# The splits of the weight tiles move from ahead of a job's post-treatment to behind it, at most four tiles ahead, in a three-block float32 network on one core

## The reference, cut to what matters

```python
def swiglu(x, w_in, w_out):
    gate, up = jnp.split(x @ w_in, 2, axis=-1)
    return (jax.nn.silu(gate) * up) @ w_out
...
    qkv = x @ w_qkv
    q, k, v = jnp.split(qkv, 3, axis=-1)
...
    for i in range(s // Q_BLOCK):
        sc = jnp.einsum('bqhmd,bkhmd->bhmqk', q[:, q0:kend], k[:, :kend],
                        preferred_element_type=jnp.float32)
        p = jax.nn.softmax(jnp.where(allowed, sc, neg), axis=-1)
        a = p[:, :, 0] - lam * p[:, :, 1]
        outs.append(jnp.einsum('bhqk,bkhe->bqhe', a.astype(v.dtype), v[:, :kend]))
```

## Time and profile before

| | |
|---|---|
| runs | 1912.24 us median of 3 (1912.19 to 1922.69) |
| profiled execution | 1916.28 us, span of the instructions 1914.6 us |
| mean granted TensorE clock | 0.984 |
| busy | PE 96%, DVE 47%, ACT 35%, POOL 3% |
| chain that ended last | PE 90%, DVE 5%, ACT 3%, issue 2% |

### The profile page before, as it was taken

How to read it: one execution, slowest core, us unless ns; L and a number is a source line. 1 busy time by engine, 2 the same in 40 slices (tenths; PEclk the granted TensorE clock), 3 DMA queues, 4 the chain that set the end, 5 groups by cost and what they waited for, 6 DMA issues and landing times.

```text
span 1914.6 us, 21555 instructions
## 1 busy us (share of the span) xinstructions
PE 1841.1 (96%) x8656; PEld 1480.3 (77%) x8656; DVE 903.6 (47%) x1544; ACT 664.8 (35%) x1084; POOL 57.9 (3%) x68
## 2 busy tenths in 40 slices
PE   8987879999999999999999999999999999999998
PEld 6755557888888897566698888888887788888886
DVE  3576766533333362555573333336544474334343
ACT  4233432422223232555432232222446444323231
POOL 0221110000000000000000000000000000000000
PEclk9989899999999999999999999999999999999999
DMA  7321111423333323222223333333321324333221
GB/s 235 98 77 49 66 53 56 132 77 112 98 99 99 120 87 107 66 67 67 83 89 99 93 95 99 99 98 96 100 73 60 110 67 122 99 100 99 77 78 44
DMA packets 217306, 174.51 MB, mean 91 GB/s; under 512 B 8899, under 2 KB 177765, under 8 KB 217206
## 3 DMA queue, kind: packets, MB, share of 16 engines
q1 hardware_dynamic: 217206, 173.13, 29.7%
HBM read 170.97 MB, written 7.38 MB: 93 GB/s over the span
## 4 chain that ended last, share of the span: by engine, by line
PE 90%; DVE 5%; ACT 3%; issue 2%; DMA 0%; SPq 0%; ACTq 0%
PE ps L526 27%; PE ps L527 27%; PE ps L528 27%; PE ps L823 2%; PE ps L783 2%; ACT whi L989 1%; PE ps L803 1%; PE ps L833 1%; PE ps L845 1%; PE ps L722 1%; DVE wlo L1263 1%; PE ps L793 0%; PE ps L934 0%; DVE arena L1289 0%; DVE arena L1285 0%
## 5 line engine op out<-in xcount | busy, mean ns | idle before, releaser
L1263 DVE TENSOR_TENSOR wlo<-raw,whi 128x1024 fp32r<-128x1024 f32 x236 | 288.3, 1225 | 588.8 <-ACT whi L989 586.6
L989 ACT ACTIVATE whi<-raw 128x1024 fp32r<-128x1024 f32 x236 | 248.8, 1059 | 578.3 <-PE ps L528 570.8
L526 PE MATMUL ps<-xh,whi 128*128 128x512 f32 (+1 forms) x1176 | 444.9, 378 | 0.0
L528 PE MATMUL ps<-xh,wlo 128*128 128x512 f32 (+1 forms) x1176 | 433.2, 368 | 0.0
L527 PE MATMUL ps<-xl,whi 128*128 128x512 f32 (+1 forms) x1176 | 433.1, 368 | 0.0
L526 PE MATMUL ps<-whi,hh 128*128 128x512 f32 x648 | 257.1, 397 | 7.2 <-DVE hl L1467 3.8
L526 PEld LDWEIGHTS ps<-xh,whi 128*128 128x128 f32 x1176 | 224.0, 190 | 39.0 <-issue 4.6
L528 PE MATMUL ps<-whi,hl 128*128 128x512 f32 x648 | 253.8, 392 | 0.0
L527 PE MATMUL ps<-wlo,hh 128*128 128x512 f32 x648 | 253.6, 391 | 0.0
L528 PEld LDWEIGHTS ps<-xh,wlo 128*128 128x128 f32 x1176 | 223.2, 190 | 37.4
L527 PEld LDWEIGHTS ps<-xl,whi 128*128 128x128 f32 x1176 | 223.6, 190 | 36.7 <-issue 2.9
(11 more groups left out here) (198 smaller groups left out, 2021.7 us busy)
## 6 DMA issues: line engine op xcount, KB each, us to landing
raw<-in_ffn_w_in SPq DMA_DIRECT2D x88, 512.0 KB, 3.9
raw<-in_w_ff SPq DMA_DIRECT2D x64, 512.0 KB, 4.0
raw<-in_ffn_w_out SPq DMA_DIRECT2D x44, 512.0 KB, 3.8
raw<-in_a_w_qkv SPq DMA_DIRECT2D x24, 512.0 KB, 5.2
raw<-in_w_in SPq DMA_DIRECT2D x20, 512.0 KB, 3.8
raw<-in_kv_w SPq DMA_DIRECT2D x16, 512.0 KB, 3.7
bias_skewed<-bias_rows SPq DMA_DIRECT2D x8, 640.0 KB
raw<-in_a_w_o SPq DMA_DIRECT2D x8, 512.0 KB, 4.7
```

What stands on the lines that cost most here:

```text
L526: e.matmul(o, ah, bh, start=start, stop=False)
L528: return e.matmul(o, al, bh, start=False, stop=stop)
L989: e.activation(self.parts(m)[0], self.raw[:, m % RAW, :], ACT.Copy).then_inc(s.hi, 1)
L1263: e.tensor_tensor(lo, self.raw[:, m % RAW, :], f32(hi), ALU.subtract).then_inc(s.lo, 1)
```

## The change

`done` no longer calls `pump`. `post` calls `pump(1)` behind its own step. The limit falls from eight tiles ahead of the last one taken (`SPLIT + EXTRA`) to four (`AHEAD`). As `slots` is a queue from which the first is taken, and as two of six slots (four of eight) are now left over, a split gets the slot that has been free the longest, mostly that of the job before the last one.

```diff
@@ -22,6 +22,7 @@
 SPLIT = 6
 EXTRA = 2
+AHEAD = 4
@@ -88,7 +89,7 @@
     def pump(self, most=2):
 
-        while most and self.slots and not self.waiting and self.n_split < len(self.tiles) + SPLIT + EXTRA:
+        while most and self.slots and not self.waiting and self.n_split < len(self.tiles) + AHEAD:
             slot, free = self.slots.pop(0)
@@ -108,7 +109,6 @@
         if self.slot_of[tile] < SPLIT or self.extra:
             self.slots.append((self.slot_of[tile], (sem, value)))
-        self.pump()
@@ -145,6 +145,7 @@
         else:
             self.step("post", job, None)
+        self.pump(1)
```

## The result

The changed kernel took 1869.99 us, the median of 4 runs (1866.1 to 1872.17), against 1914.38 us for the kernel before beside it (4 runs, 1912.19 to 1922.69): a ratio of 0.9758 [0.9722, 0.9794], faster by 44 us or 2.4%. The forecast was 1877.0 us with a range of 1862 to 1898. The profiled execution took 1871.5 us, with a span of 1869.8 us, where the one before had 1914.6 us.

What follows compares the result with a forecast made beforehand. TensorE, busy 96%, bounds the kernel; its idle time and low clock, mainly in the first attention, can be won. 25.6 + 8 - 3 + 4 = 34.6, rounded to 35 us: 1881 us profiled, 1877 us median, range 1862 to 1898.

Steps and rivals of the forecast that it cites:

- What bounds the kernel: Whole kernel: TensorE busy 96%; feed-forwards can gain nothing, the gain lies in the attentions' waits and low clock.
- The waits on the post: First attention: each post begins 2.35 us earlier, so ten waits on its last operation, 32.6 us, shrink by 21.9 us.
- The shares and maxima: First attention: two waits on the shares' L1459 shrink by 2.2 us, one on the maxima's L1126 by about 1.5.
- the splits' new places: First attention: splits beside GpSimd's addition or ahead of shares cost 3 us, about 0.2 for each of 14 jobs.
- The clock: First attention: five or six of eleven clock falls left, 1.7 us each; 9.4 us won, 8 of it real.
- The second attention: Second attention: waits on L1490 shrink and part of one clock fall goes, 4 us; shares 1.3 us later are covered.
- Fewer tiles ahead: Norms and loads: splitting four tiles before use instead of six or more costs nothing; else L526 would wait on wlo.
- the clock and the coupling keep half: Rival, chance 0.17: in the first attention each shortened wait lets the next grow; gain 15 to 20 us, about 1894.
- the wait only moved: Rival, chance 0.05: split delays the next head's maxima; first attention gains nothing, second loses 18 us and more, 1930.
- nothing comes of it: Rival, chance 0.04: post starts earlier but TensorE's waits end with another releaser at the same time, 1905 to 1915.
- GpSimd and VectorE lock each other out: Rival, chance 0.06: 11 first-attention splits each wait for GpSimd's 1.27 us addition, giving back 14 us; 1891.

Runs made afterwards that it cites:

- e3: Changed kernel with the split put back directly ahead of the post, at most five tiles ahead there, so in an older slot: 1887.18 us.
- e1: Changed kernel with the old limit of eight tiles ahead; the split stays behind the post but takes the slot just freed: 1871.38 us.
- e2: Changed kernel with only the limit of four kept; `done` calls `pump` again and `post` doesn't: 1871.86 us.
- e4: Changed kernel with each PSUM bank chosen as the one given back longest ago, instead of the next in turn: 1868.41 us.
- e7: Changed kernel with VectorE's half of every split done twice: 1941.7 us.

## Why the prediction was right, point by point

**What bounds the kernel: right.** The feed-forwards kept their length, TensorE busy throughout. All but 2.3 of the 44.8 us came in the two attentions.

**The waits on the post, 21.9 us: right.** 32.6 fell to 10.2 us, by 22.4. The price of 2.35 us per wait was 2.41 where it can be read alone (4.69 to 2.28, and 3.38 to 0.97). The three forecast to stay above 2 us did, at 2.28, 2.28 and 2.18. The reason given for the price was incomplete: it took both halves in series as one cause, and e3 shows two.

**The shares and maxima, 2.2 + 1.5, and the splits' new places, -3: right, each for itself.** The two waits on L1459 fell from 5.4 to 2.6 us, by 2.85 where 2.2 was taken, and the one on L1126 from 2.9 to 1.6, by 1.3 where 1.5 was taken. Five new waits on the shares came in their place, 3.4 us together: that is the subtraction of 3 us. In all 25.6 - 3 = 22.6 us were forecast, and TensorE's idle time fell by 23.1.

**The clock, 8 us: the mechanism right, the size wrong.** The term was forecast at 8 us and measured 12.8. The price of a fall was right (1.7 taken, about 1.5 measured). The step that failed is the count: "I take five or six falls to be left", and then 8 of 9.4 "real". In the trace of the kernel before, the eleven falls stood behind ten waits of 2.47 to 4.69 us and one of 1.89, and none behind a shorter one. My own list left three waits above 2 us and the rest under about 1.5, so it allowed three falls at most. There were two, one and one in three traces of this order.

**The second attention, 4 us: the cause right, the size too small.** It gave 6.5 us: 4.3 of idle time (7.7 to 3.4) and 2.2 of busy time. I had taken 2 of the 3.7 us of its four longer waits; nearly all went (4.9 to 0.5 in total). The cause is the one given, shares that no longer stand behind a split; but it takes the limit of four to get there, since a split right behind the post still stands ahead of them and gives only 3.3 us (e1). The 1.3 us by which the next shares come later were covered, as forecast: no wait of L834 stands there.

**The mixer: missed.** 2.1 us came that were not in the sum. One wait of 1.85 us on the mixer's hl (L1574) is 0.3 us now, which is 1.6 of them. The fall of the clock behind it (at 1518.58 us) is gone, and another stands earlier in the mixer (at 1382.27). Why that wait shrank I have not traced.

**Fewer tiles ahead, at nothing: right.** No wait of L527 on wlo stands in a feed-forward or at a norm; the one in the trace is that at the start, 3.0 us in both.

**What the change is.** The title and the first sentences on the change give the move to the call in `post`; with the limit of four the limit does it (e2). The order of the engines, from which the terms were read, was right, so no number hung on it.

**The rivals.** That the clock and the coupling keep half: no, but e4 and e7 show the coupling it feared, in the 22 us that are left. That the wait only moved: no; in the second attention L834 waits 0.5 us once. That nothing comes of it: no. That GpSimd and VectorE lock each other out: the lock is there, and its price was already being paid. GpSimd's addition in the first attention, before and then after:

```profile
L1603 POOL TENSOR_TENSOR arena<-arena 128x512 f32<-128x512 f32 x14 | 17.8, 1270 | 141.2 <-DVE arena L1289 141.2
```

```profile
L1604 POOL TENSOR_TENSOR arena<-arena 128x512 f32<-128x512 f32 x13 | 22.4, 1720 | 98.7 <-DVE arena L1290 98.6
```

In e1, where a split stands behind nearly every post, the mean is 2111 ns for each of 13. Who loses is seen in two places. In e1 the split began first, and GpSimd took 2.13 us, 0.99 us of them up to the split's end at 138.41:

```profile
137.19 1.22 DVE L1264 TENSOR_TENSOR wlo<-raw,whi 128x1024 fp32r<-128x1024 f32 x1
...
137.42 2.13 POOL L1604 TENSOR_TENSOR arena<-arena 128x512 f32<-128x512 f32 x1 [12.23 <-DVE arena L1290]
```

In the changed kernel GpSimd was once the first, by 0.05 us, and the split took 2.30 us:

```profile
103.66 1.27 POOL L1604 TENSOR_TENSOR arena<-arena 128x512 f32<-128x512 f32 x1 [0.28 <-DVE arena L1290]
103.71 2.30 DVE L1264 TENSOR_TENSOR wlo<-raw,whi 128x1024 fp32r<-128x1024 f32 x1 [0.20 <-ACT whi L990]
```

The Trainium skill (SBUF — State Buffer, "Who interferes with whom") says that the order of issue decides which of the two blocks, and that the other blocks fully. These two places agree: the later one ended 1.14 us and 1.08 us after the first had ended, near the length it has alone. The place at 83.77 in the earlier trace rows does not: GpSimd's L1608 was the first by 0.56 us there, and the split kept its 1.23 us. The prediction quoted the rule's first half and priced VectorE as the loser each time; at most places the split begins right behind the post's last operation, some 0.2 us ahead of GpSimd, which is released by that operation.

But VectorE pays one operation later. The shares' L1456 reads two operands from SBUF and takes 0.16 us alone; in four places it began while GpSimd's addition ran, took 1.05 us, and ended within 0.02 us of it:

```profile
97.74 2.13 POOL L1604 TENSOR_TENSOR arena<-arena 128x512 f32<-128x512 f32 x1 [10.64 <-DVE arena L1290]
...
98.84 1.05 DVE L1456 TENSOR_TENSOR stat<-stat,small 128x1 f32<-128x1 f32 x1
```

TensorE's wait of 1.31 us at 101.44 ends with the shares behind this row. Added up, the first attention of the changed kernel loses 4 x 0.9 us of VectorE so, 2 x 1.0 at the next line (L1457, 1.5 us instead of 0.5) and 1.1 at the one split, some 6.7 us. The kernel before lost 6 x 1.0 us at that next line (its L1456, as in the earlier trace rows). So hardly anything was given back, where the rival had 14 us.

**The total.** 34.6 us forecast, 44.8 in the profiled execution: 23.1 for 22.6, 12.8 for 8, 6.5 for 4, 2.1 for 0, and 0.3 elsewhere.

## What to carry to other kernels

Work done ahead for later use belongs behind the treatment of a result in every engine's order, and into a buffer that is free already: the place and the buffer are two separate delays. In the first attention an older buffer alone was worth 15 us and the place 21 or more beyond that, and behind the post the buffer counted for nothing (e1); in the second either was enough, if the place was behind the next results as well. A limit on how far ahead a planner works can decide both, so look at the order that comes out, not at the line that was moved. When waits are priced, count also what the clock loses behind each one that is removed, and ask whether the next result of the same engine is late by as much: giving TensorE another bank here only showed it the next late result. And when an operation is doubled to see what it costs, look up how long the second one took: here it was 1.71 us and not 1.22.

## What the runs showed of the hardware that I had not expected

A wait of 2.28 us of TensorE at the same matmul of the same order was followed by the granted clock's lower level in one execution and not in another (two, one and one falls in three traces of the changed order; none and one in two of e1's). Longer waits are not sure to be followed by one either: of the kernel before, the wait of 2.92 us that ended at 277.48 had none, and one of 1.89 us, ending at 213.72, had one. A fall costs TensorE about 1.5 us. So two orders cannot be told apart in a single trace where they differ by 3 us in a stage with such waits.

GpSimd's addition, 1.27 us alone, took 2.0 to 2.1 us in 13 of 13 cases in e1, where a split begins just ahead of it. VectorE's next operation with two operands in SBUF, 0.16 us alone, then took 1.05 us where it began during the addition (six places in e1, four in the changed kernel), and ended with it. No wait of TensorE ends with GpSimd itself, so this price shows only as a longer VectorE operation.
